# One transposition of x instead of two in a decoder layer: the turned block, unscaled, feeds both the normed activation and the residual

## What is computed

```python
h = x
u = rms_norm(h, g_mix[l])                  # x * rsqrt(mean(x*x) + EPS) * g_mix, per token
z = u @ w_in[l]                            # all projections of both mixers and of the gates
...
g_a, g_r = jnp.split(jax.nn.sigmoid(gates + b_gate[l]), 2, axis=-1)
h = h + (g_a * y_a + g_r * y_r) @ w_out[l] # x again, as the residual
...
mkv = (rms_norm(mem, g_mem[l]) @ w_xkv[l])  # keys and values of the memory rows
```

## Time and profile before

| | |
|---|---|
| runs | 1807.3, 1804.27, 1806.22 us; median 1806.22 |
| profiled execution, first to last instruction | 1807.1 us |
| PE busy | 1759.0 us (97%), 8599 matmuls and transposes |
| DVE, POOL, ACT busy | 1087.8, 982.2, 698.0 us |
| TensorE clock, mean granted | 0.993 |
| DMA | 262 MB, 145 GB/s mean |

### The profile page before, as it was taken

The page is one execution under the profiler, slowest core; times in us unless marked ns, Lnnn a source line. Parts: engine busy times, 40 slices in busy tenths (PEclk is TensorE's granted clock), DMA queues, the critical chain, the costliest instruction groups (busy, mean ns, idle before and its releaser), DMA issues.

```text
span 1807.1 us, 25034 instructions
## 1 busy us (share of the span) xinstructions
PE 1759.0 (97%) x8599; PEld 1467.8 (81%) x8599; DVE 1087.8 (60%) x1535; ACT 698.0 (39%) x1243; POOL 982.2 (54%) x554
## 2 busy tenths in 40 slices
PE   7999999999999899999999999999999999999998
PEld 7888888888888677788878888778888888878887
DVE  5655663002334778884345564887777777889842
ACT  7422223111013667731133232644444444444432
POOL 6743333445654577654433232577777777655540
PEclk9999999999999999999999999999999999999999
DMA  6511111347661789583221134243433334494322
GB/s 266 204 52 36 36 43 49 139 164 256 227 227 46 276 317 325 177 308 113 103 71 59 59 104 141 77 139 107 142 117 123 133 110 139 142 344 143 122 76 93
DMA packets 111245, 262.33 MB, mean 145 GB/s; under 512 B 7744, under 2 KB 50368, under 8 KB 106688
## 3 DMA queue, kind: packets, MB, share of 16 engines
q1 hardware_dynamic: 84720, 182.13, 30.3%
q10 hardware_dynamic: 26448, 79.18, 11.8%
HBM read 186.82 MB, written 73.92 MB: 144 GB/s over the span
## 4 chain that ended last, share of the span: by engine, by line
PE 84%; DVE 6%; ACT 5%; issue 2%; DMA 1%; POOL 1%; ACTq 0%; DVEq 0%; SPq 0%; POOLq 0%
PE ps L714 16%; PE ps L719 16%; PE ps L720 16%; PE ps L1333 7%; PE ps L1338 7%; PE ps L1335 7%; PE ps L1408 2%; PE ps L1409 2%; PE ps L1410 2%; ACT prow L1792 2%; PE ps L1110 1%; PE ps L1090 1%; DMA raw<-in_slabs 1%; DVE aneg L2570 1%; PE ps L1431 1%
## 5 line engine op out<-in xcount | busy, mean ns | idle before, releaser
L609 POOL TENSOR_SCALAR wh<-raw 128x1024 fp32r<-128x1024 f32 x75 | 211.6, 2822 | 467.3 <-PE ps L714 448.9
L714 PE MATMUL ps<-uh,wh 128*128 128x512 f32 x560 | 221.2, 395 | 0.7 <-POOL wl L602 0.7
L720 PE MATMUL ps<-uh,wl 128*128 128x512 f32 x560 | 218.4, 390 | 0.0
L719 PE MATMUL ps<-ul,wh 128*128 128x512 f32 x560 | 218.0, 389 | 0.0
L611 POOL TENSOR_TENSOR wl<-raw,wh 128x1024 fp32r<-128x1024 f32 x75 | 182.0, 2427 | 6.3
L646 POOL TENSOR_TENSOR wl<-raw,wh 128x512 fp32r<-128x512 f32 x88 | 137.5, 1573 | 69.1 <-ACT wh L1457 67.8
L633 POOL TENSOR_TENSOR over_rings<-over_rings 128x512 f32<-128x512 f32 x92 | 118.2, 1285 | 51.5 <-DMA over_rings<-in_slabs 45.9
L1457 ACT ACTIVATE wh<-raw 128x512 fp32r<-128x512 f32 (+1 forms) x164 | 105.4, 656 | 88.9 <-PE ps L1338 58.0
L689 POOL TENSOR_TENSOR wl<-raw,wh 128x512 fp32r<-128x512 f32 x63 | 93.7, 1496 | 78.2 <-ACT wh L1457 78.2
L2212 DVE SCALAR_TENSOR_TENSOR ya<-zA,sm,ya 128x512 f32<-128x512 f32 x88 | 109.6, 1246 | 31.7 <-ACT ya L2036 24.6
L720 PEld LDWEIGHTS ps<-uh,wl 128*128 128x128 f32 x560 | 105.1, 188 | 22.6
(11 more groups left out here) (488 smaller groups left out, 4873.9 us busy)
## 6 DMA issues: line engine op xcount, KB each, us to landing
raw<-in_slabs SPq DMA_DIRECT2D x110, 512.0 KB, 3.6
over_rings<-in_slabs SPq DMA_DIRECT2D x22, 1024.0 KB, 7.1
s_s<-over_rings SPq DMA_DIRECT2D x22, 1024.0 KB, 4.9
ssm<-s_s SPq DMA_DIRECT2D x22, 512.0 KB, 4.5
raw<-s_s SPq DMA_DIRECT2D x22, 512.0 KB, 3.8
s_f<-yb ACTq DMA_DIRECT2D x22, 512.0 KB, 5.3
raw<-s_d SPq DMA_DIRECT2D x36, 256.0 KB, 2.5
dsum<-in_slabs SPq DMA_DIRECT2D x16, 512.0 KB, 6.7
```

Source lines behind the costliest of these rows:

```text
L609: pool.tensor_scalar(wh[:, j, :], raw[:, j % RAWS, :], 1.0, None, ALU.mult).then_inc(S["w_hi"], 1)
L714: l = pe.matmul(o, lh, rh, start=start, stop=False)
L719: pe.matmul(o, lh, rl, start=False, stop=False)
L720: return pe.matmul(o, ll, rh, start=False, stop=stop)
```

## The change

1. In the entry x is transposed as it was loaded. DVE no longer scales the rows `xs`. The inverse norms `rst_x` are transposed instead: four transposes of a broadcast column for each half (`x_scales` on PE), which ACT copies to a tile `rbx` with the norms of 512 tokens along the free axis (`x_scale`).
2. For each block DVE now makes the scaled activation `u32` = PSUM x `g_mix` x `rbx` (`x_u`). ACT copies the unscaled PSUM block to `xst` (the residual) and `u32` to `uh`, and after each four blocks stores 1 MB of `xst` to `s_x`. DVE makes `ul` = `u32` - `uh` with both operands in SBUF.
3. The blocks are spread anew: one behind the first value group, two behind each of the next six, none behind the eighth, and the last three within the first half of the first retention product (`X_AT`, `X_LATE`). The copies of the first value half (`value_hi(0)`) wait until two of the stores have landed, since `xst` lies over their tiles.
4. The second load of x, its 16 transposed blocks, their copies and their eight stores in the gate stage go.

```diff
+X_AT = ((0,), (1, 2), (3, 4), (5, 6), (7, 8), (9, 10), (11, 12), ())
+X_LATE = (13, 14, 15)
...
-        xs, junk, ck = place(64, [("xs", [P, NT, D], 0), ("junk", [P, D], 0), ("ck", [P, T + NT * R16], 0)])
+        xs, rbx, ck = place(64, [("xs", [P, NT, D], 0), ("rbx", [P, 2, H2], 0), ("ck", [P, T + NT * R16], 0)])
+        (junk,) = place(28, [("junk", [P, D], 0)])
+        (u32,) = place(32, [("u32", [P, KB, T], 0)])
+        xst = [place(kb, [(f"xst{kb}", [P, KB, H2], 0)])[0] for kb in (137.5, 64)]
...
                 if c == 1 and i == 0:
-                    for b in range(2):
-                        pe.wait_ge(d_free[b], USE0["xv"])
+                    pe.wait_ge(S["x_std"], 5)
...
             def turn_x(n):
                 b, k = n // KB, n % KB
                 if k == 0:
-                    pe.wait_ge(S["x_row"], CH * (b + 1))
+                    for t in range(CH * b, CH * (b + 1)):
+                        pe.wait_ge(*x_landed(t))
                 if n < 4:
                     pe.wait_ge(S["mm_lo"], 2 * n + 2)
                 else:
-                    pe.wait_ge(S["xT_lo"], n - 3)
+                    pe.wait_ge(S["xT_hi"], n - 3)
...
+            def x_scales(b):
+
+                pe.wait_ge(S["x_rs"], b + 2)
+                pe.wait_ge(d_free[b], KB // 2)
+                for j in range(CH):
+                    t = CH * b + j
+                    l = pe.transpose(ps[:, b, j * P:(j + 1) * P], rst_x[:, t:t + 1].to_broadcast([P, P]), ident)
+                l.then_inc(S["row_t"], 1)
...
             for i in range(2 * SLOTS):
                 value_rows(i // SLOTS, i % SLOTS)
-                turn_x(2 * i)
-                turn_x(2 * i + 1)
+                if i in (0, 2):
+                    x_scales(i // 2)
+                for n in X_AT[i]:
+                    turn_x(n)
...
-            def x_turn(n):
-                b, k = divmod(n, KB)
...
-                for t in range(CH):
-                    l = pe.transpose(ps[:, 2 + n % 4, t * P:(t + 1) * P], xtile[:, t, k * P:(k + 1) * P], ident)
-                l.then_inc(S["mm_t"], 1)
...
             def u_ready(k, b):
                 pe.wait_ge(S["xT_lo"], KB * b + k + 1)
+                if b == 0 and k in (1, 3, 5):
+                    turn_x(X_LATE[k // 2])
...
             def x_hi(n):
                 b, k = n // KB, n % KB
-                act.wait_ge(S["xT_t"], n + 1)
+                act.wait_ge(S["x_u"], n + 1)
                 if n == 0:
                     act.wait_ge(S["mm_t"], KB // 2)
-                copy(uh[:, k, half(b)], ps[:, 4 + n % 4, :], scale=smc("g_mix", k)).then_inc(S["xT_hi"], 1)
+                if n == KB - 1:
+                    act.wait_ge(S["x_sq"], NT)
+                copy(xst[b][:, k, :], ps[:, 4 + n % 4, :])
+                copy(uh[:, k, half(b)], u32[:, k, half(b)]).then_inc(S["xT_hi"], 1)
+                if k % CH == CH - 1:
+                    act.wait_ge(S["xT_hi"], n + 1)
+                    act.dma_start(s_x[k - CH + 1:k + 1, :, half(b)].rearrange("k p n -> p k n"),
+                                  xst[b][:, k - CH + 1:k + 1, :]).then_inc(S["x_ld0" if b else "mm_ld"], 16)
+
+            def x_scale(b):
+                act.wait_ge(S["row_t"], b + 2)
+                copy(rbx[:, b, :], ps[:, b, :]).then_inc(S["x_std"], 1)
...
-                x_hi(2 * i)
-                x_hi(2 * i + 1)
-                if i == SLOTS:
+                if i == 0:
+                    x_scale(0)
+                for n in X_AT[i]:
+                    x_hi(n)
+                if i == 2:
+                    x_scale(1)
+                if i == SLOTS + 2:
+                    act.wait_ge(S["mm_ld"], 16 * MB + 32)
                     for r in range(MB):
                         value_hi(0, r)
...
-            def x_rows(b):
-
-                act.wait_ge(*((S["mm_t"], KB // 2 + KB) if b else (S["y_t"], 2 * RH)))
-                for t in range(CH):
-                    act.dma_start(xtile[:, t, :], x[(CH * b + t) * P:(CH * b + t + 1) * P, :]).then_inc(
-                        S[f"x_ld{t}"], 16)
...
-                dve.wait_ge(S["x_rs"], b + 2)
-                for t in range(CH * b, CH * (b + 1)):
-                    dve.tensor_scalar(xs[:, t, :], xs[:, t, :], rst_x[:, t:t + 1], None, ALU.mult).then_inc(
-                        S["x_row"], 1)
+
+            def x_u(n):
+                b, k = n // KB, n % KB
+                dve.wait_ge(S["xT_t"], n + 1)
+                dve.wait_ge(S["x_std"], b + 4)
+                stt(u32[:, k, half(b)], ps[:, 4 + n % 4, :], smc("g_mix", k), rbx[:, b, :], ALU.mult,
+                    ALU.mult).then_inc(S["x_u"], 1)
...
-                stt(ul[:, k, half(b)], ps[:, 4 + n % 4, :], smc("g_mix", k), uh[:, k, half(b)].bitcast(f32), ALU.mult,
-                    ALU.subtract).then_inc(S["xT_lo"], 1)
+                lo(ul[:, k, half(b)], u32[:, k, half(b)], uh[:, k, half(b)]).then_inc(S["xT_lo"], 1)
...
-                x_lo(2 * i)
-                x_lo(2 * i + 1)
-                if i == 1:
+                for n in X_AT[i]:
+                    x_u(n)
+                    if n:
+                        x_lo(n - 1)
+                if i == 0:
                     x_rows(1)
-                if i == SLOTS:
+                if i == SLOTS + 2:
                     for r in range(MB):
                         value_lo(0, r)
+            for n in X_LATE:
+                x_u(n)
+                x_lo(n - 1)
+            x_lo(2 * KB - 1)
```

More of the change, by code:

```diff
@@ L295, in build @@
         oth, otl = place(32, [("oth", [P, RH, T], 1), ("otl", [P, RH, T], 1)])
-        (xtile,) = place(120, [("xtile", [P, CH, D], 0)])
-        (xst,) = place(140, [("xst", [P, 4, 2, H2], 0)])
         (hT,) = place(0, [("hT", [P, KB, T], 0)])
@@ L403, in mix_tiles, with x_landed @@
             return (sa0, mr0) if m < 2 else (sac, mrc) if m in (4, 5) else (sab, mrb)
+        def x_landed(t):
+            return S[f"x_ld{t if t < CH else t // 2 * 2}"], 16 if t < CH else 32
         def row(t, i):
@@ L415, in build @@
         for name in ("ld0 ld1 w_hi w_kv_hi w_ready w_used par done0 done1 free0 free1 "
-                     "x_ld0 x_ld1 x_ld2 x_ld3 x_ld4 x_ld6 x_sq x_std x_rs x_row xT_t xT_hi xT_lo "
+                     "x_ld0 x_ld1 x_ld2 x_ld3 x_ld4 x_ld6 x_sq x_std x_rs x_u xT_t xT_hi xT_lo "
                      "cst angs sins "
-                     "pos_t rot_t rot t_qk qk_hi qk_lo kr_hi kr_lo rows_v v_hi v_lo s_t s_m s_hi s_lo kv_t r_st gn_rc "
+                     "row_t rot_t rot t_qk qk_hi qk_lo kr_hi kr_lo rows_v v_hi v_lo s_t s_m s_hi s_lo kv_t r_st gn_rc "
                      "r_hi r_lo y_t gn_st var std yn_done yT_t yg_done y_hi y_lo "
@@ L917, in _, with gates_and_heads @@
             for j in range(4):
[L918 to L920 removed]
+                dense(j, SLAB0["ga"] + 4 + j, USE0["ga"] + 4 + j, KB, of(uh, ul))
             pe.wait_ge(S["y_lo"], 2 * RH)
[L925 removed]
+            def gates_and_heads(i):
                 for j in range(4):
                     s, u = SLAB0["gr"] + 4 * i + j, USE0["gr"] + 4 * i + j
[L928 to L929 removed]
                     if j % 2 == 0:
[L931 removed]
+                        dense(j, s, u, KB, of(uh, ul))
                     else:
[L933 to L934 removed]
+                        dense(j, s, u, RH, of(yth, ytl))
+            gates_and_heads(0)
             for k in range(KB):
@@ L1639, in gate_a @@
                     act.dma_start(row(s_ga, m), sig[:, p, :]).then_inc(S[f"g_st{p}"], 16)
-            def x_rows(b):
-                act.wait_ge(*((S["mm_t"], KB // 2 + KB) if b else (S["y_t"], 2 * RH)))
-                for t in range(CH):
-                    act.dma_start(xtile[:, t, :], x[(CH * b + t) * P:(CH * b + t + 1) * P, :]).then_inc(
-                        S[f"x_ld{t}"], 16)
-            def x_copy(n):
-                b, k = divmod(n, KB)
-                if k == 0:
-                    act.wait_ge(*((S["mm_ld"], 16 * MB + 64) if b else (S["y_t"], 2 * RH)))
-                q = n // 2 % 4
-                for e in range(2):
-                    act.wait_ge(S["mm_t"], KB // 2 + n + e + 1)
-                    copy(xst[:, q, e, :], ps[:, 2 + (n + e) % 4, :]).then_inc(S["mm_hi"], 1)
-                act.wait_ge(S["mm_hi"], KB + n + 2)
-                act.dma_start(s_x[k:k + 2, :, half(b)].rearrange("k p n -> p k n"), xst[:, q, :, :]).then_inc(
-                    S["mm_ld"], 16)
             order(RH, lambda j, b: gate_a(j, b, j % 2), last=True)
-            x_rows(0)
             for m in range(4, KB):
@@ L1682, in gate_r @@
                                        bias=smc("b_gate", KB + m)).then_inc(d_free[b], 1)
-                        if first and p == 1:
-                            x_copy(KB + 2 * b)
-                    if first and p == 1:
-                        x_copy(KB + 4)
-                        x_copy(KB + 6)
                     for b in range(2):
```

33 lines of the change are left out of this document (9 added, 24 removed).

## The result

The changed kernel is slower: 1809.83 us (median of 18 runs, 1807.55 to 1814.24) against 1805.68 us for the kernel before (18 runs, 1803.83 to 1809.16); the ratio is 1.0023 with an interval of 1.0016 to 1.0030, or +4.15 us between the medians. The prediction said 1810.2 us and +4.0.

What follows compares the result with a forecast made beforehand. The prediction took PE, busy 97% of the span, as the bound: entry +11.0 us and gate stage -7.0 us sum to +4.0, forecast 1810.2 us, range 1803.5 to 1814.0.

Steps and rivals of the forecast that it cites:

- Gate stage: Between the gate products: removing 64 transposes from a PE that is never idle gives back 7.0 us (6.5 to 7.5).
- Entry: Up to the second retention product: it starts at 89.5 instead of 79.5 us; with the lower clock, +11.0 us.
- Blocking: Entry: DVE's `x_lo` waits out POOL's two-operand subtraction if POOL began first, POOL waits if DVE did; `TENSOR_SCALAR` costs nothing.
- Clock: First retention product: the 5.7 us wait brings half clock, costing 1.7 us, of which 1.1 shows.
- What holds the first product: End of entry: ACT copies slab 16 at 71.45, POOL ends at 75.0, product starts at 75.1 after 5.7 us idle.
- Rival B: Entry: with slab 16 copied on ACT by about 66, the first product needn't wait; down to 1798.3 us; chance 0.10.
- Stores in the entry: Entry: the 1 MB stores slow nearby slab loads; 0.1 us at 1.5 each, up to 2 us at 3.5 on two.
- Rival A: Entry: DVE and POOL pass each other; +7.0 with the clock, less 7.0 is 0.0, 1806.2 us; chance 0.20.

Runs made afterwards that it cites:

- the first experiment: Kernel before with the second transposition left out and the old entry kept; 1797.88 us, ratio 0.9961 to the kernel before.
- filled-wait run: Changed kernel plus 20 unread matmuls on PE in the wait ahead of the first retention product; 1808.24 us, ratio 1.0021 to the kernel before.
- one-operand experiment: Changed kernel with POOL making the low part of slabs 10 to 16 by a one-operand TENSOR_SCALAR; 1808.42 us, ratio 1.0016 to the kernel before.
- slab-16 run: Changed kernel with ACT copying slab 16 ahead of block 11 instead of behind block 12; 1809.32 us, ratio 1.0021 to the kernel before.
- low-part experiment: Changed kernel with the activation's low part made from the PSUM block instead of the SBUF tile; 1807.47 us, ratio 1.0014 to the kernel before.
- run without residual copies: Changed kernel without ACT's 16 copies of the unscaled block; 1807.90 us, ratio 1.0009 to the kernel before.
- run without late turns: Bank-freed run with blocks 13 to 15 transposed ahead of the first retention product; 1805.52 us, ratio 0.9998 to the kernel before.
- bank-freed run: Slab-16 run with the second value half's evacuations ahead of the first half's on ACT and DVE; 1808.27 us, ratio 1.0017 to the kernel before.

## Why the prediction held, step by step

- **Gate stage, -7.0.** This is shown: -7.14 by the trace of the first experiment, -7.0 by its ratio, and again in after, where the `g_final` transposes come at 391.57 us from group 0: +3.8, which is 10.8 - 7.0.
- **Entry, +11.0.** Measured +10.8. The waits were put at 1.9, 1.5, 5.7 and a last one for the sines; they are 1.49, 1.08, 5.24 and 1.15. Slab 16 on ACT was put at 71.45 and came at 70.52, the table load at 83.2 and came at 83.65. That the total is only 0.2 off is partly luck. The filled-wait run shows the entry without the lower clock: +9.2, where the forecast had +9.9. The clock then showed 1.55 where it had 1.1. The two misses cancel.
- **Blocking.** This is confirmed in both directions that the prediction assumed: seven of the 16 `ul` took 1.95 to 2.52 us beside POOL's subtraction, each ending 0.54 to 0.56 us after it, and where DVE began first, at 44.70, POOL's subtraction took 2.93 us. The entry is 3.3 us shorter when the second SBUF operand goes. The Trainium skill ("SBUF — State Buffer", section "Who interferes with whom") has such a DVE instruction contend with a GpSimd instruction that reads SBUF, and the order of issue decide which of the two blocks. The trace agrees for the subtractions. The one-operand experiment differs: of six `ul` that started beside a `TENSOR_SCALAR` of 2.77 us and more, none waited for its end, and the longest took 1.37. In after the one at 80.34 took 0.86 beside one of 3.22. The measurement decides, as the prediction took it.
- **Clock, 1.7 with 1.1 of it showing.** The price was too small: it measured 2.2, of which 1.55 reached the second product. The prediction took it over from 8 matmuls behind a wait of 1.93 us (0.20 us each, so 1.6), and here the lower clock lasted longer into the product.
- **What holds the first product.** Here the reasoning was incomplete; the number came right by luck, because the gate I named happened to be the later of two. In after the slab was ready at 74.01 (71.66 + 2.35) and the bank at about 72.8, when the first `mvl` of the pair at 72.11 had ended. Rival B held that a copy of slab 16 by about 66 would make the kernel faster; that falls, since at 66.06 the time was 1809.3. One after the other, by the yardstick, the slab gained nothing (0.4 longer), the bank 1.8 us, the late turns 1.3, the block kept in PSUM 4.2, and the order of the `x_lo` 2.9. Taking the blocking away by itself gave 3.3. The bank, the late turns and the order of the `x_lo` weren't tried by themselves.
- **Stores in the entry, 0 to 2 us.** These were not separated. Two slab loads took 7.6 us in the median beside `s_k` and `s_x` stores in the slab-16 run, but what waited for them was hidden behind the first product. The stores alone weren't tried.
- **Rival A (no blocking, 0.0).** What failed is its premise, for DVE and POOL do not pass each other. The low-part experiment made the premise true, and there its lists fit: the first product was put at 71.2 and came at 71.25, with group 0 0.5 us earlier than in before; the second was put at 84.8 and 1.7 for the clock, and came at 86.55. By the yardstick that entry is +7.5 against the +7.0 forecast. The time was +2.5 (0.9 to 4.0) against 0.0; the 2 us that the yardstick doesn't account for stay open.

## What to carry to other kernels

Work taken off a full engine comes back whole, but what replaces it must be priced in the order of the stage where it lands: here 7 us came back, the entry took 10.8, and the kernel was 4 us slower. When a product waits, list every semaphore in front of it with the time at which each is ready; moving the latest alone buys only the distance to the next. Before giving an SBUF home to a value that DVE reads again, look at what POOL does meanwhile. With the scaled block left in PSUM, and the order of slab 16, of the value copies, of the late turns and of the `x_lo` changed too, the same change was 6.3 us faster than the kernel before.

## What the runs showed of the hardware

- POOL's subtraction with two SBUF operands stopped a DVE subtraction with two SBUF operands until it ended; POOL's `TENSOR_SCALAR` did not, but slowed some (0.69 to 0.86 or 1.37 us). The longest `ul`, 2.86 us, was in the run without residual copies.
- The loss is a wait and does not scale with DVE's work: in the run without late turns an operation on 128x4 elements, 0.23 us in after, took as long as POOL's subtraction.

```profile
81.33 2.40 DVE L2203 SCALAR_TENSOR_TENSOR hx<-hx,cn 128x4 f32<-128x4 f32 x1
...
81.31 2.39 POOL L620 TENSOR_TENSOR wl<-raw,wh 128x1024 fp32r<-128x1024 f32 x1
```

- POOL waits too: a subtraction that began beside a running `ul` took 2.93 us (after, 44.72) and 2.42 where `ul` read PSUM (low-part run, 44.69); a `TENSOR_SCALAR` that did so took 3.22 (after, 79.17) instead of 2.77.
- DVE's subtraction from PSUM took 0.68 to 0.69 us in all 16 blocks, with POOL's subtractions beside it, and scaling in place in PSUM took 0.75 to 0.76 us, as much as to SBUF (0.74 to 0.75).
- Waits of 1.49 and 1.08 us brought no lower clock; one of 5.24 us did, and so did one of 3.93 (0.57 granted from 73 to 77 us in the bank-freed run). The waits of 2.57 and 3.31 us in the run without late turns left 70 to 90 us at 1.00, while the earlier trace rows have 0.50 behind a wait of 1.93. So the length of the wait alone doesn't settle it, and what else does stays open.
